# Three-product stick-breaking scores, with small moves around two square sums, eight decays and three normalizations

## The chip, the cores and the metric

One core of one Trainium2 chip runs the whole program. The metric is the device time of one execution in microseconds (us), lower is better. The core has TensorE (PE in the rows; its weight loads are PEld), VectorE (DVE), ScalarE (ACT), GpSimd (POOL) and SyncE (SP, which here only issues transfers). Each engine runs its own instructions in the order in which they were written; semaphores carry the dependences between engines.

## What is computed

Two blocks on 512 tokens of width 1024, batch 1, float32. The first has two sequence mixers and an MLP, the second is sparse attention (NSA). The parts near the change, cut from the reference:

```
# first block
h = rms_norm(x, norm_mix_g)
p = h @ w_in                      # q_a k_a v_a o_a i_a f_a q_b k_b v_b g_a g_b
...
qn, kn = head_rms_norm(q_b), head_rms_norm(k_b)        # 8 heads of 128
y = gates[:D] * y_a + gates[D:] * stick_breaking(qn, kn, v_b)
x = x + y @ w_out
x = x + square(relu(rms_norm(x) @ w_up)) @ w_down

def stick_breaking(q, k, v):      # per head
    z = q @ k.T / sqrt(128)       # the scores; only s < t counts
    log_keep = where(s < t, log_sigmoid(-z), 0)
    suffix   = reverse_cumsum(log_keep) - log_keep
    A = where(s < t, exp(log_sigmoid(z) + suffix), 0)
    return A @ v

# the other mixer, 8 heads of 64, has a decay per pair of positions:
#   P = exp(b_t - b_s + i_s - m_t) * (q . k)
```

The second block starts with a norm (the second of three that the change touches) and ends with an output projection whose input is turned in the same way (the third).

## The kernel before

Weights come in slabs of 1 MB (`w_raw`, two buffers) by SP. ACT writes a rounded copy of each slab (`split_hi`, L688, into `w_hi`) and DVE the remainder (`split_lo`, L696, into `w_lo`); both are in the type fp32r, which TensorE takes in one pass. Every large product is then three fp32r products: high by high, high by low, low by high. Activations are split in the same way (`act_hi`, `act_lo`). A product tile has 128 rows and 512 columns, and its two banks `ps_g` are used in turn; other work has `ps_z` and `ps_t`.

There is no scheduler. The order on each engine is the order in which the program writes it, so a wait at the head of an engine's queue holds all that stands behind it. Four places matter.

**First slabs (L1273 to L1324).** PE sums the first value slabs over eight steps (`first_step`) and then starts the next ones (`mm_half` on `N_VA + 2`), whose first tile goes to `ps_z` and needs the `act_evacuate` of the tile before (ACT, L883, `v_a<-ps_z`). ACT also makes the sums of squares of the four token blocks of x (`square_sum`, L1725), which wait for the transfers `x_sb<-in_x`. They lead over `sq_done` and DVE to `rstd`, `diag_ready` and the scaling of x.

**Decay heads (L1350 to L1391, loop over 8 heads).** Per head ACT writes `decay` (`decays`, L1780, four exponentials), POOL masks it (L2532), DVE multiplies it with the scores (L2195), and PE multiplies the result with the values (L1374). A head's slab for the next head is split in the same loop.

**Stick-breaking heads (L1418 to L1458, loop over 8 heads, `h`).** PE: the scores of head h into `ps_z` (L1428, four causal column blocks of 512, 384, 128 and 256, plain fp32), the values product of head h-1 (L1414), one gate tile of 24 products, half of the second one, the suffix sums (L1441 to L1454, from `sp_hi` and `sp_lo`), the rest of the second tile. ACT: Abs, Exp and Ln of the scores (L1860 to L1862, with a table load ahead of Ln), the rounded copy `sp_hi` (L1869), the gate's tanh (L891, table load ahead), the exponential `attn_b` (L1876), the second tanh. DVE: L2235, `sp_lo` (L2239), the gate product (L968), a minimum on `ps_z` in four parts (L2247), the gate product, and `normalize(h + 2)` (L2207), which gives the normalized q_b and k_b. Head 0 differs: PE computes its scores after three of the four tiles of the last value slab (`N_VB + 3`), and ACT has just evacuated the third of these (`v_b<-ps_g`, L883) and loaded the table of Exp (L1843).

**Three turned activations (`feature_tiles`, L782).** PE transposes four normalized token blocks (`xn` or `o_a`) into eight feature tiles of 512 columns, 128 columns per block (L789). Tiles 0 and 1 lie in `ps_g`, 2 to 7 in `ps_z` and `ps_t`. The last block is late. ACT then writes `act_hi` (`act_feature_tile`, L849) and DVE `act_lo` (`dve_feature_tile`, L862 or L860), tile by tile, and the next slab's first product needs both of tile 0.

Of the kernel before, what the change touches and what calls it, by code (L numbers as in the profile page):

```python
# [23 lines left out]
ALU = mybir.AluOpType  # L24
ACT = mybir.ActivationFunctionType
AX_X = mybir.AxisListType.X
F32 = mybir.dt.float32
F32R = mybir.dt.float32r

P = 128  # L30
# [143 lines left out]
def program(nc, a, out):  # L174

    with ExitStack() as ctx:
# [40 lines left out]
        y_lo = sb("y_lo", [P, KT, S], F32R, at=arena + 4 * K16)  # L217
        yb_f = sb("yb_f", [P, HB, S], at=arena + 3 * K16)
# [82 lines left out]
        m_bc = [sb("m_bc0", [P, S], at=tile_t_at + 2048), sb("m_bc1", [P, S], at=t1 + 7168 + 2048 * 3)]  # L301
        den_sum = sb("den_sum", [P, S - P], at=tile_t_at)
# [115 lines left out]
        b_sp = sem("b_sp")  # L418
        b_masked = sem("b_masked")
# [41 lines left out]
        gain_in = sem("gain_in")  # L461
        out_ready = sem("out_ready")
# [56 lines left out]
        BY_ACT = {"norm": 1, "conv": 1, "no": 1, "oa": 1, "ga": 1, "gb": 2, "up": 3, "nz": 1, "zw": 1}  # L519
# [23 lines left out]
        for n in range(N_ALL):  # L543
            taken_at[n] = tuple(taken)
            if n in norm_before:
                norm_tile_of[n] = len(kinds)
                take("norm")
                take("norm")
# [233 lines left out]
        def feature_tiles(pe, n, src, block_ready, between=None, before=None, late=None, halves=False):  # L782
# [4 lines left out]
            def turn(b, ks):  # L787
                for k in ks:
                    mm = nc.tensor.transpose(feature_bank(n, k)[:, b * P:(b + 1) * P],  # L789
                                             src(b)[:, k * P:(k + 1) * P], ident)  # L790
                    if b == TB - 1:
                        mm.then_inc(tile_ready if k < 2 else norm_done, 1)

            for j in range(TB - 1):
                block_ready(j)
                if j == 0 and before is not None:

                    wait_tile_free(pe, tile_of[before])
                    wait_tile_free(pe, tile_of[before] + 1)
                if late is None:  # L800
# [11 lines left out]
            for k in (0, 1):  # L812
                wait_bank(pe, t0 + k)
                for j in range(TB - 1):
                    turn(j, (k,))
            block_ready(TB - 1)
            turn(TB - 1, range(HALF_K))
# [24 lines left out]
        def act_feature_tile(act, n, k, which, gain):  # L842

            if k < 2:
# [3 lines left out]
            scale = 1.0 if gain is None else col(gain, k)  # L848
# [3 lines left out]
        def dve_feature_tile(dve, n, k, which, gain):  # L852
            t = norm_tile_of[n] + k
            if k < 2:
                after_act(dve, t, 1)
# [396 lines left out]
        def _(pe):  # L1252
# [165 lines left out]
            for h in range(HB):  # L1418
# [6 lines left out]
                pe.wait_ge(b_normed, 2 * h + 2)  # L1425
                for b in (0, 1, 3, 2):
                    at, w = CAUSAL_AT[b], CAUSAL_W[b]
                    mm = nc.tensor.matmul(ps_z[:, at:at + w], k_b[:, h, b * P:(b + 1) * P],  # L1428
                                          q_b[:, h, b * P:S], start=(b != 3), stop=True,
                                          skip_group_check=True)  # L1430
# [277 lines left out]
        def _(act):  # L1708
# [28 lines left out]
            for b in range(2):  # L1737
                square_sum(b)
            act_evacuate(act, N_VA + 1, 0)
            act_evacuate(act, N_VA + 1, 1)  # L1740
            square_sum(2)
            act_evacuate(act, N_VA + 1, 2)
            act_evacuate(act, N_VA + 1, 3)
# [990 lines left out]
```

## Time and profile before

| | |
|---|---|
| median of 3 runs | 1310.84 us (1310.53 to 1311.0) |
| the profiled execution | 1312.24 us |
| its span, first to last instruction | 1310.5 us |
| PE busy | 1297.0 us, 99% |
| DVE busy | 766.7 us, 59% |
| ACT busy | 690.2 us, 53% |
| POOL busy | 194.7 us, 15% |
| DMA | 130.72 MB, mean 100 GB/s |

An engine's busy share tells how much of the span it had an instruction in work. Matmuls are pipelined, so a product's duration is longer than the step to the next product's start; how long PE works is read from starts. The profiled execution took 1.4 us more than the median, and 1.7 us of it lie outside the span.

### The profile page before, as it was taken

To read this page: it belongs to the slowest core of one execution; us is meant where nothing else is said; L and a number is where in the kernel's file an instruction comes from. 1 tells how busy PE (TensorE), PEld (TensorE's weight loads), DVE (VectorE), ACT (ScalarE), POOL (GpSimd) and SP (SyncE) were. 2 spreads that over 40 slices of the span, in tenths; PEclk is the share of its full clock that TensorE was granted. 3 is DMA by queue.
4 is the path that set the end of the run, shared out by engine and by line. 5 is a ranking of instruction groups with operands and counts; after the bars stand their busy time and mean duration, and the time that the engine had idled before them with its cause. 6 is when DMAs were issued, how large, how long until landed. Compare 5 with 4: busy or idle time off the path is not lost.

```text
span 1310.5 us, 16447 instructions
## 1 busy us (share of the span) xinstructions
PE 1297.0 (99%) x6464; PEld 1055.5 (81%) x6464; DVE 766.7 (59%) x1184; ACT 690.2 (53%) x1070; POOL 194.7 (15%) x260
## 2 busy tenths in 40 slices
PE   8999999999999999999999999999999999999998
PEld 7787777787778887888888888788888888888886
DVE  4696443435544545595775958822157778786553
ACT  5547555357676334554635546544335667675332
POOL 0002332151000000000000000003712333431000
PEclk9999999999999999999999999999999999999999
DMA  8333221464111234143070430372612122231311
GB/s 311 90 107 119 81 81 65 111 189 120 65 41 56 97 97 165 60 142 115 1 250 8 150 107 1 97 229 81 142 35 79 60 96 73 67 104 52 118 65 65
DMA packets 64444, 130.72 MB, mean 100 GB/s; under 512 B 3999, under 2 KB 33695, under 8 KB 60272
## 3 DMA queue, kind: packets, MB, share of 16 engines
q1 hardware_dynamic: 58320, 110.81, 25.1%
q0 software_dynamic: 5904, 18.81, 5.9%
q8 instruction: 52, 0.85, 0.3%
q14 instruction: 24, 0.20, 0.1%
q10 hardware_dynamic: 144, 0.06, 0.0%
HBM read 126.77 MB, written 2.88 MB: 99 GB/s over the span
## 4 chain that ended last, share of the span: by engine, by line
PE 94%; DMA 2%; DVE 1%; issue 1%; ACT 0%; POOL 0%; SPq 0%; DVEq 0%; POOLq 0%
PE ps_g L728 39%; PE ps_g L751 16%; PE ps_z L751 7%; PE ps_t L1500 7%; PE ps_z L1500 5%; PE ps_z L1611 3%; PE ps_z L1649 3%; PE ps_t L1683 3%; PE ps_z L1428 1%; PE ps_t L1414 1%; PE ps_t L1374 1%; PE ps_t L1533 1%; DMA x_sb<-in_x 1%; PE ps_z L1454 1%; DMA w_raw<-in_w_in_t 1%
## 5 line engine op out<-in xcount | busy, mean ns | idle before, releaser
L728 PE MATMUL ps_g<-act_hi,w_hi 128*128 128x512 f32 x760 | 299.1, 394 | 1.3 <-DVE act_lo L862 0.9
L728 PE MATMUL ps_g<-act_hi,w_lo 128*128 128x512 f32 x760 | 296.0, 390 | 0.0
L728 PE MATMUL ps_g<-act_lo,w_hi 128*128 128x512 f32 x760 | 295.8, 389 | 0.0
L696 DVE TENSOR_TENSOR w_lo<-w_raw,w_hi 128x2048 fp32r<-128x2048 f32 x80 | 182.6, 2283 | 192.9 <-ACT w_hi L688 192.5
L688 ACT ACTIVATE w_hi<-w_raw 128x2048 fp32r<-128x2048 f32 x80 | 152.3, 1904 | 88.1 <-PE ps_g L751 47.9
L728 PEld LDWEIGHTS ps_g<-act_hi,w_hi 128*128 128x128 f32 x760 | 142.7, 188 | 32.6 <-issue 4.1
L728 PEld LDWEIGHTS ps_g<-act_hi,w_lo 128*128 128x128 f32 x760 | 142.7, 188 | 30.1
L728 PEld LDWEIGHTS ps_g<-act_lo,w_hi 128*128 128x128 f32 x760 | 142.8, 188 | 28.5
L751 PE MATMUL ps_g<-w_hi,act_hi 128*128 128x512 f32 x264 | 107.0, 405 | 0.7 <-DVE act_lo L860 0.7
L751 PE MATMUL ps_g<-w_hi,act_lo 128*128 128x512 f32 x264 | 103.2, 391 | 0.0
L751 PE MATMUL ps_g<-w_lo,act_hi 128*128 128x512 f32 x264 | 102.7, 389 | 0.0
L2625 POOL TENSOR_SCALAR cmp_in_k<-pairk,vec 128x124 f32<-128x124 f32 x16 | 13.5, 864 | 491.2 <-ACT pairk L917 491.2
L2007 ACT ACTIVATE probs<-probs,rneg 128x128 f32<-128x128 f32 (+3 forms) x128 | 70.4, 552 | 7.7 <-DVE rneg L2446 7.5
L688 ACT ACTIVATE w_hi<-down_raw 128x2048 fp32r<-128x2048 f32 x24 | 46.1, 1919 | 50.9 <-PE ps_t L1500 29.2
L696 DVE TENSOR_TENSOR w_lo<-down_raw,w_hi 128x2048 fp32r<-128x2048 f32 x24 | 55.0, 2290 | 8.0 <-ACT w_hi L688 8.0
L2645 POOL TENSOR_TENSOR q_parts<-qn,q_parts 64x512 fp32r<-64x512 f32 x32 | 41.3, 1289 | 117.6 <-ACT q_parts L1987 117.1
L899 ACT ACTIVATE ev_t<-ps_g 128x512 f32<-128x512 f32 x32 | 19.1, 597 | 74.9 <-PE ps_g L728 74.9
L751 PEld LDWEIGHTS ps_g<-w_hi,act_lo 128*128 128x128 f32 x264 | 49.5, 188 | 10.9
L751 PEld LDWEIGHTS ps_g<-w_hi,act_hi 128*128 128x128 f32 x264 | 49.7, 188 | 9.9 <-issue 1.1
L751 PEld LDWEIGHTS ps_g<-w_lo,act_hi 128*128 128x128 f32 x264 | 49.8, 188 | 9.1
L2442 DVE CUSTOM_DVE_ANT_0 probs<-ps_z,tile_t 128x128 f32<-128x128 f32 (+3 forms) x128 | 55.0, 485 | 3.1 <-PE ps_z L1611 3.1
L981 DVE TENSOR_TENSOR up_lo<-up_raw,up_hi 128x256 fp32r<-128x256 f32 (+1 forms) x32 | 17.8, 557 | 54.9 <-ACT up_hi L904 54.9
(389 smaller groups left out, 2486.9 us busy)
## 6 DMA issues: line engine op xcount, KB each, us to landing
w_raw<-in_w_in_t SPq DMA_DIRECT2D x30, 1024.0 KB, 4.9
w_raw<-in_nsa_w_in SPq DMA_DIRECT2D x20, 1024.0 KB, 5.1
w_raw<-in_w_up SPq DMA_DIRECT2D x16, 1024.0 KB, 5.5
down_raw<-in_w_down SPq DMA_DIRECT2D x16, 1024.0 KB, 5.3
tile_t<-bias_rev_dram POOLq DMA_DIRECT2D x32, 256.0 KB, 3.1
bc<-stat_rows_dram POOLq DMA_DIRECT2D x24, 256.0 KB, 6.3
w_raw<-in_w_out SPq DMA_DIRECT2D x4, 1024.0 KB, 5.1
w_raw<-in_nsa_w_out SPq DMA_DIRECT2D x4, 1024.0 KB, 5.0
```

The costliest lines, as they stand in the source:

```text
L688: nc.scalar.activation(slab_view(parts(n)[0], n), slab_view(raw(n), n), ACT.Copy).then_inc(hi_done, 1)
L696: nc.vector.tensor_tensor(slab_view(lo, n), slab_view(raw(n), n), slab_view(hi, n).bitcast(F32), ALU.subtract).then_inc(lo_done, 1)
L728: mm = nc.tensor.matmul(o, stationary, moving, start=(k == 0 and j == 0), stop=(k == KT - 1 and j == 2))
L751: mm = nc.tensor.matmul(bank(t), act[:, k, m], w[:, k - k0, :], start=(k == 0 and j == 0), stop=(k == KT - 1 and j == 2))
L899: nc.scalar.activation(ev_t[:, g, :], ps_g[:, g, :], ACT.Relu).then_inc(ev_act, 1)
L1500: mm = nc.tensor.matmul(down_bank(p, i), act[:, k, m], w[:, k, :], start=(first and k == 0 and j == 0), stop=(k == HALF_K - 1 and j == 2), ...
L1611: mm = nc.tensor.matmul(ps_z[:, at:at + w], q_parts[u % 2][:, b * P:(b + 1) * P], keys[u // 4 % 2][:, 0:w], start=(j == 0), stop=(j == 1))
L1649: mm = nc.tensor.matmul(ps_z[64 * e:64 * e + 64, CAUSAL + at * P:CAUSAL + 2 * P], values[:, s, g * DH:(g + 1) * DH], blocks[:, first:last: ...
L1683: mm = nc.tensor.transpose(ps_t[:, at:at + P], probs[u % 2][:, ROWS_AT[b] + s * P:ROWS_AT[b] + (s + 1) * P], ident)
L2007: ins = nc.scalar.activation(p, p, ACT.Exp, bias=rneg[:, u % 2, b:b + 1], accum_out=rsum[:, u % 2, b:b + 1])
L2442: ins = nc.vector.tensor_tensor_reduce(probs[u % 2][:, at:at + w], ps_z[:, at:at + w], tile_t[u % 2][:, S - w:S], 1.0, -3.0e38, ALU.add, A ...
L2645: nc.gpsimd.tensor_tensor(q_parts[u % 2][64 - half:128 - half, :], qn[half:half + 64, 4 * (h // 8) + h % 4, :], q_parts[u % 2][half:half + ...
```

## The change

It has four parts.

1. **Scores.** The normalized q_b and k_b of a head are split into fp32r parts (`qk_hi` on ACT into two new tiles `q_b_hi` and `k_b_hi`; `qk_lo` on DVE, in place of q_b and k_b), and the scores become three fp32r products per column block in place of one fp32 product. PE waits for `b_qk_lo` where it waited for `b_normed`. In the same loop the weight splits move: ACT's from the start of a head to behind `sp_hi`, DVE's to behind the minimum.
2. **First values.** ACT's four evacuations of the first value tiles stand between the square sums, the first of them ahead of all.
3. **Decays ahead of splits.** In decay heads 1 to 7 ACT writes the decays before it splits the next slab, and DVE multiplies them before its part of the split.
4. **Norm tiles in two pieces.** Feature tile 0's first three blocks are turned earlier; ACT copies these 384 columns while the last block is still missing, and the last 128 afterwards. PE waits for the first copy before it writes the last block.

```diff
@@ tiles and tables @@
+        q_b_lo = sb("q_b_lo", [P, HB, S], F32R, at=arena + 3 * K16)
+        k_b_lo = sb("k_b_lo", [P, HB, S], F32R, at=arena + 4 * K16)
+        q_b_hi = sb("q_b_hi", [P, S], F32R, at=tile_t_at)
+        k_b_hi = sb("k_b_hi", [P, S], F32R, at=tile_t_at + 2048)
-        BY_ACT = {"norm": 1, "conv": 1, "no": 1, "oa": 1, "ga": 1, "gb": 2, "up": 3, "nz": 1, "zw": 1}
+        BY_ACT = {"norm0": 2, "norm": 1, "conv": 1, "no": 1, "oa": 1, "ga": 1, "gb": 2, "up": 3, "nz": 1, "zw": 1}
...
@@ feature_tiles (PE) @@
+                if j == TB - 2:
+
+                    wait_bank(pe, t0)
+                    for i in range(TB - 1):
+                        mm = turn(i, (0,))
+                    mm.then_inc(norm_early, 1)
...
-            for k in (0, 1):
-                wait_bank(pe, t0 + k)
-                for j in range(TB - 1):
-                    turn(j, (k,))
+            wait_bank(pe, t0 + 1)
+            for j in range(TB - 1):
+                turn(j, (1,))
             block_ready(TB - 1)
+            after_act(pe, t0, 1)
             turn(TB - 1, range(HALF_K))
...
@@ act_feature_tile (ACT) @@
+            if k == 0:
+
+                act.wait_ge(norm_early, which)
+                nc.scalar.activation(act_hi[:, k, 0:S - P], feature_bank(n, k)[:, 0:S - P], ACT.Copy,
+                                     scale=scale).then_inc(ev_act, 1)
+                tile_done(act, norm_tile_of[n])
+                nc.scalar.activation(act_hi[:, k, S - P:S], feature_bank(n, k)[:, S - P:S], ACT.Copy,
+                                     scale=scale).then_inc(ev_act, 1)
+                return
...
@@ stick-breaking heads (PE) @@
-                pe.wait_ge(b_normed, 2 * h + 2)
+                pe.wait_ge(b_qk_lo, 2 * h + 2)
                 for b in (0, 1, 3, 2):
                     at, w = CAUSAL_AT[b], CAUSAL_W[b]
-                    mm = nc.tensor.matmul(ps_z[:, at:at + w], k_b[:, h, b * P:(b + 1) * P],
-                                          q_b[:, h, b * P:S], start=(b != 3), stop=True,
-                                          skip_group_check=True)
+                    keys, queries = slice(b * P, (b + 1) * P), slice(b * P, S)
+                    for j, (k, q) in enumerate(((k_b_hi[:, keys], q_b_hi[:, queries]),
+                                                (k_b_hi[:, keys], q_b_lo[:, h, queries]),
+                                                (k_b_lo[:, h, keys], q_b_hi[:, queries]))):
+                        mm = nc.tensor.matmul(ps_z[:, at:at + w], k, q, start=(b != 3 and j == 0), stop=(j == 2),
+                                              skip_group_check=True)
...
@@ first values (ACT) @@
-            for b in range(2):
-                square_sum(b)
             act_evacuate(act, N_VA + 1, 0)
+            square_sum(0)
             act_evacuate(act, N_VA + 1, 1)
+            square_sum(1)
             square_sum(2)
             act_evacuate(act, N_VA + 1, 2)
+            square_sum(3).then_inc(sq_done, 1)
             act_evacuate(act, N_VA + 1, 3)
-            square_sum(3).then_inc(sq_done, 1)
...
@@ decay heads (ACT; DVE's split_lo moves in the same way) @@
-                split_hi(act, n + 1)
                 if h:
                     act.wait_ge(a_ssq, h)
                     decays(h)
+                split_hi(act, n + 1)
...
@@ stick-breaking heads (ACT) @@
+            def qk_hi(h):
+
+                act.wait_ge(b_normed, 2 * h + 2)
+                if h:
+                    act.wait_ge(b_z, h)
+                for src, dst in ((q_b, q_b_hi), (k_b, k_b_hi)):
+                    nc.scalar.copy(dst[:], src[:, h, :]).then_inc(b_hi, 1)
+
+            qk_hi(0)
             for h in range(HB):
                 n = N_OA + h
-                if h:
-                    split_hi(act, n + 1)
...
-                if h == 0:
-                    split_hi(act, n + 1)
+                split_hi(act, n + 1)
                 act_evacuate(act, n, 0)
+                if h + 1 < HB:
+                    qk_hi(h + 1)
                 act.wait_ge(b_min, h + 1)
...
@@ stick-breaking heads (DVE) @@
+            def qk_lo(h):
+                for e, (src, dst, hi) in enumerate(((q_b, q_b_lo, q_b_hi), (k_b, k_b_lo, k_b_hi))):
+                    dve.wait_ge(b_hi, 4 * h + e + 1)
+                    nc.vector.tensor_tensor(dst[:, h, :], src[:, h, :], hi[:].bitcast(F32), ALU.subtract)\
+                        .then_inc(b_qk_lo, 1)
+
+            qk_lo(0)
```

On ACT, at the entry to the stick-breaking heads, this stands before (`v_b` is a value tile's evacuation, `rstd<-cst` a one-element Exp that loads the table, `sp_t<-ps_z` the Abs of head 0):

```order
L883 ACTIVATE v_b<-ps_z 128x512 [waits tile_ready] x2
L883 ACTIVATE v_b<-ps_g 128x512 [waits tile_ready]
L1843 ACT_TABLE_LOAD
L1843 ACTIVATE rstd<-cst 1x1
L1860 ACTIVATE sp_t<-ps_z 128x1280 [waits stats_out,b_z,act_order]
```

and this now:

```order
L905 ACTIVATE v_b<-ps_z 128x512 [waits tile_ready] x2
L905 ACTIVATE v_b<-ps_g 128x512 [waits tile_ready]
L1868 ACT_TABLE_LOAD
L1868 ACTIVATE rstd<-cst 1x1
L1880 CAST q_b_hi<-q_b 128x512 [waits b_normed,act_order]
L1880 CAST k_b_hi<-k_b 128x512
L1892 ACTIVATE sp_t<-ps_z 128x1280 [waits stats_out,b_z]
```

The two copies of head 0 stand behind the evacuation of the third value tile and the table load, ahead of the Abs.

On DVE, from head 0's gate product to head 1's `L2235` (`ps_z<-ps_z,cst` is the minimum, `w_lo` the split of a slab), this stands before:

```order
L968 SCALAR_TENSOR_TENSOR y_f<-ev_t,y_f 128x512 [waits a_y,ev_act]
L2247 TENSOR_TENSOR ps_z<-ps_z,cst 128x128 [waits b_sfx]
L2247 TENSOR_TENSOR ps_z<-ps_z,cst 128x128 x3
L968 SCALAR_TENSOR_TENSOR y_f<-ev_t,y_f 128x512 [waits a_y,ev_act]
L2207 SCALAR_TENSOR_TENSOR q_b<-q_b,gq_s,bc_89 128x512 [waits bc_in4]
L2207 SCALAR_TENSOR_TENSOR k_b<-k_b,vec,bc_90 128x512 [waits bc_in5]
L696 TENSOR_TENSOR w_lo_56<-w_raw_52,w_hi_54 128x2048 [waits hi_done]
```

and this now:

```order
L990 SCALAR_TENSOR_TENSOR y_f<-ev_t,y_f 128x512 [waits a_y,ev_act]
L2281 TENSOR_TENSOR ps_z<-ps_z,cst 128x128 [waits b_sfx]
L2281 TENSOR_TENSOR ps_z<-ps_z,cst 128x128 x3
L2261 TENSOR_TENSOR q_b_lo<-q_b,q_b_hi 128x512 [waits b_hi]
L2261 TENSOR_TENSOR k_b_lo<-k_b,k_b_hi 128x512 [waits b_hi]
L702 TENSOR_TENSOR w_lo_57<-w_raw_53,w_hi_55 128x2048 [waits hi_done]
L990 SCALAR_TENSOR_TENSOR y_f<-ev_t,y_f 128x512 [waits a_y,ev_act]
```

Between the minimum and the second gate product there are now the two remainders for the next head's scores and the slab's split.

## Rows read from the trace of the kernel before

**Rows 1.** The page: busy time of each engine, and the chain's shares.

```profile
PE 1297.0 (99%) x6464; PEld 1055.5 (81%) x6464; DVE 766.7 (59%) x1184; ACT 690.2 (53%) x1070; POOL 194.7 (15%) x260
...
PE 94%; DMA 2%; DVE 1%; issue 1%; ACT 0%; POOL 0%; SPq 0%; DVEq 0%; POOLq 0%
```

**Rows 2.** Waits of PE: total us, times, longest us.

```profile
PE ps_g L728 <- DVE act_lo L862: 1.8, 2, 0.9
PE ps_g L751 <- DVE act_lo L860: 0.7, 1, 0.7
```

**Rows 3.** Timeline, first values: start us, us, engine, line, operation, [idle before].

```profile
29.29 1.07 ACT L883 ACTIVATE v_a<-ps_z 128x512 f32<-128x512 f32 x2
...
28.26 0.39 PE L1273 MATMUL ps_g<-w_lo,act_hi 128*128 128x512 f32 x1
30.02 0.47 PE L751 MATMUL ps_z<-w_hi,act_hi 128*128 128x512 f32 x1 [1.36 <-ACT v_a L883]
```

**Rows 4.** Timeline, decay head 1: ACT, DVE, PE.

```profile
121.28 1.92 ACT L688 ACTIVATE w_hi<-w_raw 128x2048 fp32r<-128x2048 f32 x1
...
127.64 1.49 DVE L2195 SCALAR_TENSOR_TENSOR decay<-ps_z,decay 128x1280 f32<-128x1280 f32 x1 [2.12 <-POOL decay L2532]
...
128.30 0.39 PE L728 MATMUL ps_g<-act_hi,w_lo 128*128 128x512 f32 x1
129.19 0.70 PE L1374 MATMUL ps_t<-decay,v_a 128*128 128x512 f32 x1 [0.51 <-DVE decay L2195]
```

**Rows 5.** Timeline of PE, head 1: the scores and the values behind them.

```profile
295.62 2.32 PE L1428 MATMUL ps_z<-q_b,k_b 128*128 128x512 f32 x8
297.78 2.32 PE L1414 MATMUL ps_t<-attn_b,v_b 128*128 128x512 f32 x8
```

**Rows 6.** Timeline of PE: suffix sums of head 1, fp32r pieces.

```profile
308.15 0.39 PE L1441 MATMUL ps_z<-sp_hi,tri_r 128*128 128x512 f32 x1
...
308.60 0.51 PE L1447 MATMUL ps_z<-sp_hi,tri_r 128*128 128x384 f32 x3
...
309.70 0.57 PE L1447 MATMUL ps_z<-sp_lo,tri_r 128*128 128x384 f32 x3
```

**Rows 7.** Timeline at the entry to head 0: PE, then ACT.

```profile
277.04 2.32 PE L1428 MATMUL ps_z<-q_b,k_b 128*128 128x512 f32 x8
...
277.24 0.60 ACT L883 ACTIVATE v_b<-ps_g 128x512 f32<-128x512 f32 x1 [2.12 <-PE ps_g L751]
277.86 1.28 ACT L1843 ACT_TABLE_LOAD   x1
...
279.45 1.24 ACT L1860 ACTIVATE sp_t<-ps_z 128x1280 f32<-128x1280 f32 x1
```

**Rows 8.** Two lines' instructions: ns min/median/max, first and last start.

```profile
L1731 ACT CAST act_hi<-x_t x8: 609/618/621, 45.6 to 61.4; 128x512 fp32r<-128x512 f32 x8
...
L2109 DVE TENSOR_TENSOR act_lo<-x_t,act_hi x8: 678/682/692, 46.8 to 62.1; 128x512 fp32r<-128x512 f32 x8
```

**Rows 9.** Timeline, second part of head 1: ACT, DVE, PE.

```profile
308.31 0.60 ACT L891 ACTIVATE ev_t<-ps_g 128x512 f32<-128x512 f32 x1
311.99 1.24 ACT L1876 ACTIVATE attn_b<-ps_z 128x1280 f32<-128x1280 f32 x1 [3.08 <-DVE ps_z L2247]
...
311.06 0.89 DVE L2247 TENSOR_TENSOR ps_z<-ps_z,cst 128x128 f32<-128x128 f32 x4 [1.42 <-PE ps_z L1454]
...
313.64 2.32 PE L1428 MATMUL ps_z<-q_b,k_b 128*128 128x512 f32 x8
```

**Rows 10.** Timeline of ACT, first norm: tiles 0 and 1.

```profile
514.55 1.27 ACT L849 ACTIVATE act_hi<-ps_g,vec 128x512 fp32r<-128x512 f32 x2 [1.41 <-PE ps_g L789]
```

**Rows 11.** Timeline of PE at both ends; windows with granted clock (PEclk), DMA, GB/s.

```profile
1.75 4.27 PE L1299 MATMUL ps_t<-k_diag 128*128 128x128 f32 x20 [1.75 <-DVE k_diag L2082]
...
1304.70 0.39 PE L751 MATMUL ps_z<-w_hi,act_lo 128*128 128x512 f32 x1
...
1309.40:1310.50 1.10, 0.00 (x0) 0.00 (x0) 0.00 (x0) 0.00 (x0) 0.00 (x0) 0.50 0.22 82
```

More of the change, by code:

```diff
@@ L418, in program @@
         b_sp = sem("b_sp")
+        b_qk_lo = sem("b_qk_lo")
         b_masked = sem("b_masked")
@@ L461, in program @@
         gain_in = sem("gain_in")
+        norm_early = sem("norm_early")
         out_ready = sem("out_ready")
@@ L546, in program @@
                 norm_tile_of[n] = len(kinds)
-                take("norm")
+                take("norm0")
                 take("norm")
@@ L792, in turn @@
                         mm.then_inc(tile_ready if k < 2 else norm_done, 1)
+                return mm
             for j in range(TB - 1):
@@ L842, in act_feature_tile @@
         def act_feature_tile(act, n, k, which, gain):
+            scale = 1.0 if gain is None else col(gain, k)
+            if k == 0:
[6 more added lines that the diff above has]
+                return
             if k < 2:
@@ L847, in act_feature_tile @@
                 act.wait_ge(norm_done, 6 * (which - 1) + k - 1)
-            scale = 1.0 if gain is None else col(gain, k)
             nc.scalar.activation(act_hi[:, k, :], feature_bank(n, k), ACT.Copy,
@@ L854, in dve_feature_tile @@
             if k < 2:
-                after_act(dve, t, 1)
+                after_act(dve, t, 2 - k)
             else:
@@ L2190, in _ @@
             for h in range(HA):
-                if h:
-                    split_lo(dve, N_QB + h + 1)
                 dve.wait_ge(a_scores, h + 1)
@@ L2196, in _ @@
                                                ALU.mult).then_inc(a_probs, 1)
-                if h == 0:
-                    split_lo(dve, N_QB + h + 1)
+                split_lo(dve, N_QB + h + 1)
                 if h < HA - 1:
@@ L2226, in _ @@
             split_lo(dve, N_OA)
+            def qk_lo(h):
[4 more added lines that the diff above has]
+            qk_lo(0)
             for h in range(HB):
                 n = N_OA + h
-                if h:
-                    split_lo(dve, n + 1)
                 dve.wait_ge(b_ln, h + 1)
@@ L2237, in _ @@
                 for p, part in enumerate(SP_PARTS):
-                    dve.wait_ge(b_hi, 2 * h + p + 1)
+                    dve.wait_ge(b_hi, 4 * h + 2 + p + 1)
                     nc.vector.tensor_tensor(sp_lo[:, part], sp_t[:, part], sp_hi[:, part].bitcast(F32),
                                             ALU.subtract).then_inc(b_lo, 1)
-                if h == 0:
-                    split_lo(dve, n + 1)
                 dve_evacuate(dve, order, n, 0)
@@ L2248, in _ @@
                 ins.then_inc(b_min, 1)
+                if h + 1 < HB:
+                    qk_lo(h + 1)
+                split_lo(dve, n + 1)
                 dve_evacuate(dve, order, n, 1)
```

## The prediction, written before the change was run

> **What bounds the kernel now.** I read the page first: PE is busy in 99% of the span, and the chain that ended last runs through PE for 94% of it [rows 1]. So only two things count: what PE's own instructions take, and the few places where PE stands still. The view of PE's waits names these places. Two kinds concern the change: the wait for `act_lo` behind the turned activations, 1.8 us in two places and 0.7 us in one [rows 2], and two single waits that the timeline shows better, since a product's duration covers some 0.16 us of a gap. One product of 512 columns follows the next by 0.225 us (308.15 to 308.60 is two of them [rows 6]). In the first values the last product of one group starts at 28.26 and the next at 30.02 [rows 3], so PE stood still for 1.76 - 0.23 = 1.53 us. In decay head 1 the step is 128.30 to 129.19 [rows 4], a stall of 0.66 us. DVE and ACT are loaded by half. They matter where PE waits for them, or where the change makes PE wait.
>
> **First values.** PE waits there for ACT's first evacuation, which starts at 29.29 [rows 3], behind two square sums. Its tile was ready long before: PE ends the four tiles three products at a time, so the first tile's last product began nine products before 28.26, at 26.2. With the evacuation ahead of the square sums it is done by about 27.3, before PE wants the bank. The second evacuation now waits for one square sum, but PE needs that bank only one tile and one small group later. The stall goes whole: **-1.5 us**. What is next late there? The diagonal of rstd, which hangs on the last square sum; that sum comes no later than now, since an evacuation moves from ahead of it to behind it. If the DMA or a later wait took the gain back it would be 0; it cannot be more than 1.53.
>
> **Decays.** In decay head 1 ACT splits a slab from 121.28 for 1.92 us [rows 4] and only then comes to the decays. POOL's mask and DVE's product follow, and DVE ends at 127.64 + 1.49 = 129.13, where PE waits. With the split behind, that chain is 1.9 us earlier and the 0.66 us are covered. Heads 2 to 7 have no gap there, since head 1 alone carries a table load in this chain, so nothing more is won. The split moves back by about 3 us, but its slab is wanted a whole head later, which hides it. **-0.65 us**, between 0 and -0.66.
>
> **Norm tiles.** The first product behind the turned blocks waits for ACT and DVE of tile 0. ACT's two copies of 512 columns take 1.27 together, the first from 514.55 [rows 10]. With 384 columns copied ahead, ACT has 128 left. ACT takes 0.618 us for 512 columns [rows 8] and 1.24 for 1280 [rows 9], 0.0008 us a column, so 384 fewer save 0.31 us. DVE's part stays whole. Three places: **-0.95 us**. PE's new wait, ahead of the last block's transposes, holds nine of its instructions; the first three blocks' copy (about 0.6 us) starts when three early transposes are done and runs beside nine others of 0.11 us each, so it ends about where PE asks. Bounds: 0 if that wait costs 0.3 each time, -1.0 if nothing.
>
> **Scores.** Now 295.62 to 297.78, 2.16 us a head [rows 5]. In future: three products of 512 columns, 0.675 us, and nine of 384, 128 and 256, 2304 columns. The nearest row is the suffix sums' nine pieces of fp32r, 2048 columns from 308.60 to 309.70, 1.10 us [rows 6]; with 256 columns more at 0.225/512 each it is 1.21. Together 1.89 us, 0.27 less a head, for eight heads **-2.2 us**. By columns alone it would be 3840 x 0.00044 = 1.69 us (-3.8 us in all); if the short pieces cost so much that nothing is won, 0. I take the middle, since the row is of the same shape and type.
>
> **The price of the parts, head 0.** This is the step that decides. PE now starts head 0's scores at 277.04 and waits for nothing [rows 7]. In the change they need `b_qk_lo`: two copies on ACT and two subtractions on DVE. The order shows the copies behind ACT's evacuation of the third value tile. That tile is PE's very last work ahead of the scores, so the evacuation starts only at 277.24, and the table load stands behind it from 277.86 for 1.28 us [rows 7]. ACT is free at about 279.4 (it starts the Abs at 279.45). Then: two copies of 512 columns at 0.618 [rows 8], overlapping by 0.1, to 280.55; the second subtraction at 0.68 [rows 8] starts behind the first and ends at 281.35; PE starts at about 281.45. Behind the waiting instruction on PE stands everything, the fourth value tile and the first gate tile among it, though neither needs the scores. A stall of 281.45 - 277.04 = **+4.4 us**, between 4.1 and 4.7. Nothing later in head 0 gives it back, since all its waits hang on the scores.
>
> The Trainium skill (ScalarE: Activation LUTs, "What ACT_TABLE_LOAD costs") gives a table switch 1283 ns for the load and some 1380 ns more for a drain. The trace shows the load alone at this place, since the next evacuation ends just ahead of it and the Abs starts 0.31 us behind it [rows 7]; by the page's sum the stall would be 5.8 us and the time 1311.4.
>
> **The price of the parts, heads 1 to 7.** Two copies (1.14 us) and two subtractions (1.3 us) a head lie on ACT and DVE beside PE. In head 1 ACT's tanh starts at 308.31; the slab's split of 1.92 us [rows 4] now comes ahead of it, less 0.4 because the Abs no longer waits behind a split, so it starts at about 309.8 and ends at 310.4. The copies follow to 311.6, in time for the exponential, which starts at 311.99 [rows 9]. DVE's gate product (0.7 us) behind the tanh ends at 311.1, where the minimum starts at 311.06 [rows 9]. All of PE's work comes 0.27 us earlier, so the minimum is late by 0.1 to 0.3. It takes 0.89, then the exponential 1.24 and, on DVE, the subtractions 1.3: both end about 313.2 to 313.4 in this head's time, and PE wants them at 313.64 - 0.27 = 313.37 [rows 9]. It is a tie. I take **+0.1 us** for the seven heads, between 0 and 0.3 each.
>
> **Sum.** -1.5 - 0.65 - 0.95 - 2.2 + 4.4 + 0.1 = -0.8 us. The profiled execution of before took 1312.24 with a span of 1310.5, 1.4 above the median of its three runs; the sum is made in its span, so I expect a span of 1309.7, and on the median 1310.84 - 0.8 = **1310.0 us**.
>
> **Rivals.**
>
> *Faster: no stall at head 0.* The scores' parts would have to be ready by 277.04, and the rest of the sum gives 1310.84 - 5.2 = 1305.6. Against it stands the order on ACT, which no dependence can change. Chance 6%.
>
> *Clock.* In this trace PE's granted clock is 1.00 until just before 1309.40, where it is 0.50; PE's last product began at 1304.70, so it fell some 4.3 us after PE had ended [rows 11]. The stall at head 0 is about as long. At the kernel's start the twenty warm-up pieces took 4.27 us [rows 11], most of it at the lower level; if the clock falls in the stall, a similar stretch of products runs at half speed and loses up to 1.9 us: 1311.9. The Trainium skill (TensorE: Matmul & The Clock Gate, Part 1) has idleness as what throttles the engine and activity as what releases it; by that rule this rival is real. Chance 18%, and within 0.2% of before.
>
> *Slower: the tie is lost in heads 1 to 7.* One mechanism: ACT's split ahead of the tanh ends late, DVE's gate product then holds the minimum, and both the exponential and the remainders come behind PE's demand. It speaks for it that four estimates meet within 0.2 us; against it, that the Abs starts earlier. Beyond 0.5 us a head it adds 3.5 us and the kernel is slower by over 0.2%; at 0.6 us a head the time is 1310.0 + 4.1 = 1314.1. Chance 8%.
>
> *First values give nothing back.* The 1.5 us stall reappears at the scaling of x or at a slab's transfer, and the time is 1311.5. Against it: everything between 30 and 60 us waits for PE. Chance 6%.
>
> **How the numbers follow.** Forecast 60%, clock 18%, slower tie 8%, first values 6%, faster 6%, something else 2%. A difference of 0.2%, 2.6 us, is about what a measurement of this kernel can tell from no change. Forecast, clock and first values lie within it: same 0.84. Faster 0.07: the first rival and a tail of the scores' lower bound. Slower 0.09: the tie, and the clock with part of it. Range 1308.2 to 1312.1: below, the scores by columns alone (-1.6 more); above, the clock's 1311.9 and the ties of 0.3 us a head (1310.0 + 2.0).
>
> **What would show it.** In the profile after: PE's wait for `v_a` at 30 us and for `decay` in head 1 are gone. The first product of each norm waits about 0.6 and 0.4 us, not 0.9 and 0.7. The scores start to values start is 1.9 us. PE has a wait of some 4.4 us for `k_b_lo` near 275 us, which would be its longest, and none above 0.3 us in heads 1 to 7. The clock is below 1.00 behind that wait in the second rival. The prediction is wrong if that wait is under 3 us, or if a second wait of over 1 us appears anywhere.

## The result, and the profile after

The changed kernel takes **1312.95 us** (median of 20 runs, 1312.61 to 1314.2); the kernel before, on the same chip, 1310.92 (20 runs, 1310.12 to 1312.37). The ratio is 1.0015 (95% interval 1.0009 to 1.0021): about 2.0 us slower. Forecast were 1310.0 us and a range of 1308.2 to 1312.1, so the time lies outside the range, and it moved the other way: +2.0 where -0.8 was forecast. It is still within the 0.2% that the prediction called no change.

The profiled execution took 1314.2 us with a span of 1312.5, the longest of the 20; the half-clock stretch below accounts for that (experiment 8 has a second look). First the page of the changed kernel (busy times and shares, then the chain that ended last), which answers to [rows 1]:

```profile
span 1312.5 us, 16560 instructions
PE 1297.3 (99%) x6496; PEld 1061.0 (81%) x6496; DVE 775.4 (59%) x1200; ACT 700.4 (53%) x1089; POOL 202.9 (15%) x260
PE 97%; DVE 1%; ACT 1%; issue 0%; DMA 0%; DVEq 0%; SPq 0%; ACTq 0%
```

PE is still busy for 99% of the span, and the page alone would say that nothing happened. The view of PE's waits says more (us in total, times, longest); it answers to [rows 2]:

```profile
PE ps_z L1454 <- DVE k_b_lo L2261: 4.3, 1, 4.3
PE ps_t L1321 <- DVE k_diag L2115: 1.8, 1, 1.8
PE ps_g L734 <- DVE act_lo L884: 1.1, 2, 0.6
PE ps_g L795 <- DVE xn L1099: 1.0, 2, 0.6
PE ps_z L1295 <- ACT act_hi L1742: 0.5, 1, 0.5
PE ps_g L757 <- DVE act_lo L882: 0.4, 1, 0.4
```

The waits for `act_lo` fell from 1.8 and 0.7 us to 1.1 and 0.4, as forecast. Those for `v_a` and for the decay are gone. On top stands the new one, 4.3 us for `k_b_lo`. The timeline of PE, ACT and DVE at that place (start, duration, instruction, and in brackets the idle time before it) answers to [rows 7]:

```profile
274.32 0.39 PE L757 MATMUL ps_g<-w_hi,act_lo 128*128 128x512 f32 x1
274.75 0.60 ACT L905 ACTIVATE v_b<-ps_g 128x512 f32<-128x512 f32 x1 [2.12 <-PE ps_g L757]
275.36 1.28 ACT L1868 ACT_TABLE_LOAD   x1
276.66 0.20 ACT L1868 ACTIVATE rstd<-cst 1x1 f32<-1x1 f32 x1
276.89 0.62 ACT L1880 CAST q_b_hi<-q_b 128x512 fp32r<-128x512 f32 x1
277.42 0.61 ACT L1880 CAST k_b_hi<-k_b 128x512 fp32r<-128x512 f32 x1
277.54 0.69 DVE L2261 TENSOR_TENSOR q_b_lo<-q_b,q_b_hi 128x512 fp32r<-128x512 f32 x1 [6.65 <-ACT q_b_hi L1880]
278.15 0.69 DVE L2261 TENSOR_TENSOR k_b_lo<-k_b,k_b_hi 128x512 fp32r<-128x512 f32 x1
278.98 0.76 PE L1454 MATMUL ps_z<-q_b_hi,k_b_hi 128*128 128x512 f32 x1 [4.27 <-DVE k_b_lo L2261]
279.55 0.63 PE L1454 MATMUL ps_z<-q_b_lo,k_b_hi 128*128 128x512 f32 x1
279.97 0.63 PE L1454 MATMUL ps_z<-q_b_hi,k_b_lo 128*128 128x512 f32 x1
```

The chain is the one the prediction wrote down, link by link: evacuation, table load, two copies, two subtractions. PE's last product is at 274.32 instead of 276.82, since this execution is 2.5 us ahead by then; the next could have followed 0.23 later and comes at 278.98, a stall of 4.43. DVE had waited 6.65 us for ACT. Note the last three rows: scores of 512 columns follow each other by 0.57 and 0.42 us and last 0.76, 0.63 and 0.63. In head 1 the first two of them start at 300.28 and 300.51 and last 0.39 and 0.40. The windows view tells why (PE busy, PEld, DVE, ACT, POOL with instruction counts, then the granted clock, the DMA share and GB/s):

```profile
275.00:278.00 3.00, 0.00 (x0) 0.00 (x0) 0.46 (x1) 2.94 (x5) 3.00 (x5) 1.00 0.97 220
278.00:279.00 1.00, 0.02 (x1) 0.05 (x1) 0.84 (x2) 0.03 (x1) 0.05 (x1) 0.73 0.97 397
279.00:280.00 1.00, 1.00 (x3) 0.81 (x4) 0.00 (x0) 0.00 (x0) 0.00 (x0) 0.50 0.98 406
...
284.00:285.00 1.00, 1.00 (x4) 0.81 (x3) 0.00 (x0) 0.97 (x2) 0.00 (x0) 0.50 0.03 12
285.00:286.00 1.00, 1.00 (x5) 0.78 (x5) 0.00 (x0) 0.98 (x2) 0.00 (x0) 0.85 0.00 0
```

The granted clock is 0.50 (1.2 GHz) from 278.5 (0.73 is the mean of a microsecond in which it falls at 0.46) to 285.3, 6.8 us. It fell while PE had been idle for some 3.9 us. Of that stretch 6.3 us hold products, each at half speed: about 3.1 us lost. This is the rival "Clock", in this execution at more than its price of 1.9.

### The profile page after: what moved, and what is told of

It is laid out like the page before. It is cut to its first block, busy times and chain, and to the rows that moved or that the text cites. A ratio compares the mean times of both kernels' runs of the same rounds, so it can differ in the third digit from the quotient of the medians.

```text
span 1312.5 us, 16560 instructions
## 1 busy us (share of the span) xinstructions
PE 1297.3 (99%) x6496; PEld 1061.0 (81%) x6496; DVE 775.4 (59%) x1200; ACT 700.4 (53%) x1089; POOL 202.9 (15%) x260
## 4 chain that ended last, share of the span: by engine, by line
PE 97%; DVE 1%; ACT 1%; issue 0%; DMA 0%; DVEq 0%; SPq 0%; ACTq 0%
PE ps_g L734 40%; PE ps_g L757 16%; PE ps_z L757 7%; PE ps_t L1525 7%; PE ps_z L1525 5%; PE ps_z L1636 3%; PE ps_z L1674 3%; PE ps_t L1708 3%; PE ps_z L1454 1%; PE ps_t L1436 1%; PE ps_t L1396 1%; PE ps_t L1558 1%; PE ps_z L1479 1%; PE ps_z L1384 1%; PE ps_z L1295 1%; PE ps_g L1295 1%
```

## The experiments

Two questions were open. Is the low clock the stall's doing, or that of the new products? And the profiled executions, one against the other, show every part's gain; do the medians show it too?

**1. Remove the stall, keep the rest.** On ACT and on DVE, head 0's copies and remainders go ahead of the slab's split; their inputs are ready long before, for DVE ends the second head's normalization at 262.8 us.

```diff
+            qk_hi(0)
             split_hi(act, N_OA)
             for i in (0, 1, 2):
                 act_evacuate(act, N_VB + 3, i)
...
-            qk_hi(0)
...
+            qk_lo(0)
             split_lo(dve, N_OA)
-            qk_lo(0)
```

> The changed kernel with head 0's two copies on ACT moved ahead of the split of the slab N_OA, and its two subtractions on DVE moved ahead of the same slab's remainder; nothing else differs. The stall theory: PE's 4.4 us wait ahead of head 0's scores is gone, and with it the 6.8 us at granted clock 0.5 that the changed kernel shows behind it. All parts keep what they gave (first values -1.6, decay -0.66, norms -0.96, scores 8 x -0.27): 1310.9 - 5.4 = 1305.5 us, clock 1.00 throughout. Rival A (the low clock near 280 us comes from the new kind of products, not from the idle time): the stall goes, the slow stretch stays, 1305.5 + 2.8 = 1308.3. Rival B (the loss is spread over heads 1 to 7 or the norms): 1308.5 with no slow stretch.

Measured: **1306.73 us** (1306.47 to 1307.43), ratio 0.9965 (0.9951 to 0.9979) against 1310.98 for before on this chip. No wait for `k_b_lo`, and the granted clock is 1.00 behind the place:

```profile
276.00:278.00 2.00, 2.00 (x14) 1.88 (x13) 0.00 (x0) 1.94 (x4) 2.00 (x4) 1.00 0.91 170
278.00:280.00 2.00, 2.00 (x11) 1.65 (x10) 0.00 (x0) 1.97 (x2) 0.95 (x2) 1.00 0.99 379
```

The same scores now run at full clock, so rival A (the kind of product) falls. This kernel beats both others. In the early place the two remainders last 1.77 us each on DVE, not 0.69, and nothing waits for them. Yet the time is 1.2 us above the 1305.5 that the parts should give, and that was not expected.

**2. The scores alone.** The kernel before with the scores' part of the change: this core and all the splits, copies and subtractions that go with it.

```diff
-                pe.wait_ge(b_normed, 2 * h + 2)
+                pe.wait_ge(b_qk_lo, 2 * h + 2)
...
-                    mm = nc.tensor.matmul(ps_z[:, at:at + w], k_b[:, h, b * P:(b + 1) * P],
-                                          q_b[:, h, b * P:S], start=(b != 3), stop=True,
-                                          skip_group_check=True)
+                    for j, (k, q) in enumerate(((k_b_hi[:, keys], q_b_hi[:, queries]),
+                                                (k_b_hi[:, keys], q_b_lo[:, h, queries]),
+                                                (k_b_lo[:, h, keys], q_b_hi[:, queries]))):
```

> The kernel before with the scores' part of the change alone. Stall theory: scores 8 x -0.27 = -2.2, stall +4.4, lost clock behind it about +2.8: 1310.9 + 5.0 = 1315.9 us, with a clock of 0.5 for 6 to 7 us behind the wait for k_b_lo. Rival A (low clock from the kind of product) gives the same total; its low clock would also show behind the scores of other heads. Rival C (the clock fell only because PE came to that place 3 us earlier in the changed kernel): full clock, 1310.9 + 2.2 = 1313.1.

Measured: 1315.68 us (1315.23 to 1316.14), ratio 1.0033 (1.0020 to 1.0046), 4.7 above before. In its profiled execution the clock is at 0.50 again behind the stall:

```profile
280.00:282.00 2.00, 2.00 (x6) 1.71 (x7) 0.00 (x0) 0.00 (x0) 0.00 (x0) 0.50 0.99 395
```

So this part, alone, costs 4.7 us as the change has it. The clock falls though none of the other parts brings PE to the place early (its last product before is at 275.23, 0.9 us later than in the changed kernel), so rival C falls too.

**3. The three other parts alone.** The changed kernel with all of the above undone (the same diff the other way round).

> The changed kernel with the scores' part undone: first values, decays and norm tiles alone. By the sum of what the trace of the changed kernel shows: -1.6 - 0.66 - 0.96 = -3.2, so 1307.7 us, clock 1.00 throughout. If one of the three parts costs something elsewhere that the traces did not show (a later wait, the transfer of a slab), 1308.5 or more.

Measured: 1308.83 us (1308.34 to 1309.24), ratio 0.9982 (0.9973 to 0.9991): 2.15 us won, where 3.2 were expected. The missing 1.1 us are those missing in experiment 1 too. Against experiment 1, same chip, the scores give 1306.73 - 1308.83 = -2.10, as forecast (-2.2). So what falls short is among first values, decays and norms.

**4. Fill the stall.** In head 0 PE gets 18 products whose sums are overwritten.

```diff
+                if h == 0:
+                    for _ in range(18):
+                        nc.tensor.matmul(ps_z[:, 0:512], tri_r[:], act_hi[:, 0, :], start=True, stop=True,
+                                         skip_group_check=True)
                 pe.wait_ge(b_qk_lo, 2 * h + 2)
```

> The changed kernel with 18 extra products of 512 columns on PE ahead of its wait for head 0's parts; their sums are overwritten by the scores, which start their banks anew. 18 x 0.227 = 4.1 us of the 4.4 us stall are filled, and nothing else moves: the scores start at the same time. Stall theory with the clock as its second price: the clock stays at 1.00, the time is 1305.5 + 4.4 = 1309.9 us, 3.0 below the changed kernel. Rival A (low clock from the kind of product): the slow stretch stays and the time is that of the changed kernel, 1312.9. Rival D (ACT and DVE hold the scores back for another reason than their queues, and the extra products push them further): above 1313.

Measured: 1311.36 us (11 runs, 1310.65 to 1311.69), ratio 1.0000 (0.9992 to 1.0009). The scores start as late as in the changed kernel (278.8 against 278.98), and the clock stays up:

```profile
278.00:279.00 1.00, 0.89 (x4) 0.43 (x4) 0.73 (x2) 0.00 (x0) 0.00 (x0) 1.00 1.01 422
279.00:280.00 1.00, 1.00 (x6) 0.87 (x6) 0.00 (x0) 0.00 (x0) 0.00 (x0) 1.00 0.97 401
```

This takes the two prices apart. The stall itself is 1311.36 - 1306.73 = 4.6 us (4.4 to 4.5 in the traces); the clock is 1312.95 - 1311.36 = **1.6 us** on the median, or 2.0 if one goes by the two ratios, since the chips differed. All 20 runs of the changed kernel are above 1312.6, and all 11 of this one below 1311.7, so by the times the clock falls in every execution; both profiled executions of the changed kernel show it (experiment 8 is the second). But 1.6 is half of what the profiled execution had lost.

**5. The first values alone.**

```diff
-            for b in range(2):
-                square_sum(b)
             act_evacuate(act, N_VA + 1, 0)
+            square_sum(0)
             act_evacuate(act, N_VA + 1, 1)
+            square_sum(1)
             square_sum(2)
             act_evacuate(act, N_VA + 1, 2)
+            square_sum(3).then_inc(sq_done, 1)
             act_evacuate(act, N_VA + 1, 3)
-            square_sum(3).then_inc(sq_done, 1)
```

> The kernel before with the first values' part alone (each evacuation on ACT ahead of the square sums that stood in front of it). Theory P (what was predicted): the 1.53 us stall near 30 us is in every execution and the part gives 1.5: ratio 0.9988, 1309.4 us. Theory V (the stall depends on when x_sb arrives): the profiled execution of before had x_sb at 26.96 and a stall of 1.53, the scores' kernel, whose first values are those of before, had it at 25.61 and a gap of under 0.3. Then the part gives 1.5 in some executions and next to nothing in the others, on the median 0.3 to 0.8: 1310.2 to 1310.7, with a narrower spread of its times than before's 2.0 us, since the upper ones of them go. By the runs so far: the three other parts together gave 2.15, less 0.66 and 0.96 leaves 0.5.

Measured: 1310.78 us (11 runs, 1310.18 to 1311.18) against 1311.22 (21 runs, 1310.27 to 1314.93), ratio 0.9994 (0.9985 to 1.0003). It gives 0.4 on the median. The interval of the ratio, -2.0 to +0.4 us, excludes neither nothing nor 1.5; the single runs say more. Those with the part lie within 1.0 us, from 1310.18. Those of before spread over 2.1 from 1310.27 up to 1312.35, and one is at 1314.93. A part that won 1.5 in every execution would have moved the lowest time too, and it moved by 0.1; the part takes away the upper ones.

**6. Fill half of the stall.** As experiment 4 with 9 products, so that 2.3 us stay idle (`range(9)`).

> As the run with 18 extra products ahead of PE's wait, with 9: 2.04 us of the stall are filled and some 2.4 us stay idle. The scores start at the same time. If the clock falls with any idle stretch of this size, the time is that of the changed kernel, 1312.9. If a stretch of 2.4 us doesn't bring it down, it is that of the 18 products, 1311.4, with clock 1.00 behind it. Between the two (falls in some executions) 1312.

Measured: 1312.73 us (1311.17 to 1313.28), ratio 1.0009 (1.0000 to 1.0018). Three of the 11 runs are at 1311.2 to 1311.7, where those with 18 products are, and eight at 1312.4 to 1313.3, where those of the changed kernel are. The profiled execution (1311.17) is one of the three, and its clock is 1.00 from 276 to 282:

```profile
278.00:280.00 2.00, 1.09 (x5) 0.96 (x6) 0.85 (x2) 0.05 (x1) 0.00 (x0) 1.00 0.96 369
```

None of the eight was profiled, but the mean clock recorded with each is 0.997 to 0.999, and that of the three 0.999 or 1.0. So, by times and mean clocks, an idle stretch of 2.3 us brings the clock down in some executions and not in others; one of 4.4 us did in all.

**7. The kernel before, once more.** No edit.

> The kernel before, unchanged, for a second look at its first 35 us. Theory V: where x_sb arrives by 25.7, PE's step near 30 us is 0.3 or less and the span is 1308.7 to 1309.3; where it arrives near 26.9 the step is 1.76 and the span near 1310.5. Theory P: step 1.76 whatever the arrival.

Measured: 1311.18 us, span 1309.4. ACT's timeline in this execution, and behind it PE's step, answer to [rows 3]:

```profile
25.86 1.06 ACT L1725 ACTIVATE xn<-x_sb 128x1024 f32<-128x1024 f32 x1 [0.88 <-DMA x_sb<-in_x]
28.17 1.07 ACT L883 ACTIVATE v_a<-ps_z 128x512 f32<-128x512 f32 x2
28.25 0.39 PE L1273 MATMUL ps_g<-w_lo,act_hi 128*128 128x512 f32 x1
28.90 0.47 PE L751 MATMUL ps_z<-w_hi,act_hi 128*128 128x512 f32 x1 [0.26 <-ACT v_a L883]
```

In the execution that the prediction read, the same square sum starts later, and the evacuation with it, at 29.29 [rows 3]:

```profile
26.96 1.06 ACT L1725 ACTIVATE xn<-x_sb 128x1024 f32<-128x1024 f32 x1 [2.32 <-DMA x_sb<-in_x]
```

In experiment 2, whose first values are those of before, it starts earlier than in both:

```profile
25.61 1.06 ACT L1733 ACTIVATE xn<-x_sb 128x1024 f32<-128x1024 f32 x1 [2.47 <-DMA x_sb<-in_x]
28.24 0.39 PE L1278 MATMUL ps_g<-w_lo,act_hi 128*128 128x512 f32 x1
28.47 0.47 PE L756 MATMUL ps_z<-w_hi,act_hi 128*128 128x512 f32 x1
```

All three end PE's first group at 28.24 to 28.26. What differs is when the transfer of `x_sb` lets ACT begin: at 25.61, 25.86 and 26.96, and PE's step is 0.23 (no stall), 0.65 and 1.76 us. The stall is the transfer's arrival, passed on by the two square sums. What counts is when it arrives, not how long ACT has waited: the execution without a stall has the longest wait, 2.47 us. The second look at before ends 1.06 us earlier than the first, and at 28.90 it is 1.12 ahead.

**8. The changed kernel, once more.** No edit.

> The changed kernel, unchanged, for a second look at the clock behind the stall. Its profiled execution was the longest of 20 (1314.2 against a median of 1312.95) with 6.83 us at granted clock 0.5. If the low stretch has one length, it is 6.8 us again and the span is near 1312.5; if its length varies, a span near 1311.1 goes with 3 to 4 us of low clock, worth 1.5 to 1.9 us, and then the clock is worth about 1.6 on the median, as the difference to the run with 18 extra products says (1312.95 - 1311.36).

Measured: 1312.83 us, span 1311.1. The same windows as above:

```profile
278.00:279.00 1.00, 0.00 (x0) 0.00 (x0) 0.92 (x2) 0.11 (x1) 0.00 (x1) 1.00 1.01 389
279.00:280.00 1.00, 0.94 (x4) 0.79 (x5) 0.00 (x0) 0.00 (x0) 0.00 (x0) 0.81 1.01 397
280.00:281.00 1.00, 1.00 (x5) 1.00 (x4) 0.00 (x0) 0.00 (x0) 0.00 (x0) 0.50 1.03 361
...
283.00:284.00 1.00, 1.00 (x6) 0.76 (x5) 0.00 (x0) 0.97 (x2) 0.00 (x0) 0.98 0.26 94
```

The same stall, but the clock falls at 279.6, when PE is already at work again, and is back at 283.0: 3.4 us at half speed, 1.7 us lost, not 3.1. The spans differ by 1.4 us. From PE's last value product ahead of head 0's scores to head 1's first score it is 24.59 us here (274.41 to 299.00), 22.99 in experiment 4 (274.21 to 297.20) and 25.96 in the first look (274.32 to 300.28): 1.6 and 3.0 us for the clock. So the price of the clock has more than one size in the same kernel, and the smaller one fits the median.

**9. Work of its own in the stall.** The fourth value tile needs none of the parts and comes ahead of PE's wait.

```diff
+                if h == 0:
+                    mm_half(pe, N_VB + 3, 3)
                 pe.wait_ge(b_qk_lo, 2 * h + 2)
...
                 if h:
                     sb_values(h - 1)
-                else:
-                    mm_half(pe, N_VB + 3, 3)
```

> The changed kernel with the fourth value tile's 12 products (2.72 us), which needs none of the scores' parts, ahead of PE's wait in head 0 instead of behind the scores. The scores start at the same time, so the stall falls from 4.4 to 1.7 us and nothing else moves: -2.7. Clock theory: an idle stretch of 2.4 us let the clock fall in most executions but not in all (the run with 9 extra products), one of 0.3 us in none; with 1.7 it falls seldom, so another -1.6 on the median: 1312.95 - 2.7 - 1.6 = 1308.6 us. If it falls in every execution: 1310.2.

Measured: 1310.77 us (11 runs, 1310.15 to 1311.02), ratio 0.9994 (0.9985 to 1.0003): 2.2 us above what was expected. The clock is not it, 1.00 throughout in the profiled execution. PE's waits between 270 and 300 us tell:

```profile
PE ps_z L1456 <- DVE k_b_lo L2261: 1.5, 1, 1.5
PE ps_z L1472 <- DVE sp_lo L2275: 0.7, 1, 0.7
PE ps_g L734 <- ACT v_b L905: 0.4, 1, 0.4
PE ps_z L1456 <- ACT attn_b L1909: 0.2, 1, 0.2
```

The stall went to 1.6 (the 1.5 of this view and what a product's duration covers), nearly the 1.7 expected, and three waits came up behind it: two in the same head, and one ahead of head 1's scores. They show 1.3 us here and cost 2.1: from the third value tile's last product to head 1's scores it is 22.25 us (274.12 to 296.37) against 18.52 in experiment 1 (275.02 to 293.54), 3.7 more, of which 1.6 are the first stall. That is nearly the whole 2.2. The value tile had been the cover under which ACT and DVE turned head 0's scores into `sp`. Moved ahead of the scores it fills one hole and leaves another.

**10. The tie in heads 1 to 7.** Experiment 1's kernel with the next slab's split at the start of these heads again, as before has it, on ACT and DVE.

```diff
             for h in range(HB):
                 n = N_OA + h
+                if h:
+                    split_hi(act, n + 1)
                 act.wait_ge(b_z, h + 1)
...
-                split_hi(act, n + 1)
+                if h == 0:
+                    split_hi(act, n + 1)
                 act_evacuate(act, n, 0)
```

> The kernel without the stall (copies and remainders of head 0 early), with the split of the next slab on ACT and DVE put back to the start of heads 1 to 7, where the kernel before has it. It prices the tie that was forecast for these heads. In the trace of the kernel without the stall the last of head 1's exponential and remainders ends at 311.07 and PE asks near 311.3, so there is 0.2 to 0.3 us to spare. The split (1.92 us) ahead of the Abs delays ACT's chain by about 0.4 us and DVE's by about as much: PE then waits 0.1 to 0.3 us a head, +0.7 to +2 in all, 1307.4 to 1308.7. If the heads have more slack than that reading says: 1306.7, no wait for attn_b or k_b_lo.

Measured: 1306.9 us (1306.57 to 1307.14), ratio 0.9967 (0.9955 to 0.9979), the same as experiment 1. PE waits for nothing between 270 and 450 us. The heads have more slack than the forecast's four close estimates said, and in heads 1 to 7 moving the split was not needed.

**11. Decays and norms alone.** The kernel before with these two parts; for the decays:

```diff
             for h in range(HA):
                 n = N_QB + h
-                split_hi(act, n + 1)
                 if h:
                     act.wait_ge(a_ssq, h)
                     decays(h)
+                split_hi(act, n + 1)
```

> The kernel before with the decays' and the norms' parts alone. By the traces: -0.66 (decay head 1) and 3 x -0.32 (norms), -1.6 us, ratio 0.9988, in every execution, since neither hangs on a transfer: the spread of before, 2 us, stays. If the median gain of the first values is near 0.4, as their run alone showed, this and that run together give the 2.15 of all three.

Measured: 1309.37 us (11 runs, 1308.45 to 1310.16), ratio 0.9987 (0.9979 to 0.9996): -1.6 us as expected, and before's spread stays, 1.7 us. With the first values' 0.4 that makes 2.0 of the 2.15 of experiment 3. Its first values are again those of before, and `x_sb` comes early:

```profile
24.79 1.06 ACT L1742 ACTIVATE xn<-x_sb 128x1024 f32<-128x1024 f32 x1 [1.40 <-DMA x_sb<-in_x]
```

PE's step there is 0.23 us (28.17 to 28.40). So of four profiled executions with the old order two had no stall, one 0.4 us and one 1.5; in all nine with the new order the step is 0.22 or 0.23.

## Why the prediction was wrong, point by point

**Two steps failed.** The first values' term, -1.5, measured -0.4; and the sum has no term for the clock, which cost 1.6 to 2.0 us. The forecast is 2.95 us low by the two together. Either alone would have left the time inside the range: 1311.1 with the first, 1311.6 to 1312.0 with the second.

**Which engine and which places: right.** PE bounds both kernels, and the wait behind ACT's table load came where and as it was described.

**First values, -1.5: the term that was mis-sized.** Profile against profile it came out (-1.6 by 28.42, where the second group begins in the changed kernel, against 30.02 [rows 3]). On the median it is -0.4. The step that failed is the one that took a stall from one execution and put it, whole, against the median: "The stall goes whole". That execution took 1312.24, 1.4 above its median. The prediction named this difference and then subtracted on the median as if every execution had the same stall. The trace held the warning, a wait on a transfer at the root of the stall (the row of experiment 7 with 2.32 us for `x_sb`), but the prediction read only the evacuation's row and not what ACT had waited for. Error: 1.1 us. The intervals of the single experiments are about as wide as this error; what carries it is that experiments 1, 3, 5 and 11 agree on the medians, and the four traces with the old order.

**Decays -0.65 and norms -0.95: right.** In the traces -0.66 and three times -0.32; together -1.6 in experiment 11. In the changed kernel's decay head 1 the split (122.80) comes behind the decays and PE is not held (compare [rows 4]):

```profile
120.97 1.93 ACT L1805 ACTIVATE decay<-m_bc,u_col 128x512 f32<-128x512 f32 x4
122.80 1.90 ACT L694 ACTIVATE w_hi<-w_raw 128x2048 fp32r<-128x2048 f32 x1
124.11 1.49 DVE L2226 SCALAR_TENSOR_TENSOR decay<-ps_z,decay 128x1280 f32<-128x1280 f32 x1 [9.30 <-POOL decay L2569]
126.80 2.32 PE L1396 MATMUL ps_t<-decay,v_a 128*128 128x512 f32 x8
```

**Scores, -0.27 a head: right.** In the changed kernel's next head they start at 300.28 and the values at 302.20, 1.92 us where [rows 5] had 2.16. Head 1's period is 17.77 us (300.28 to 318.05) where it was 18.02, 0.25 shorter; experiments 1 and 3 give -2.1 for the eight. The suffix sums' short pieces were the right row to cost short products by; by columns alone it would have been 1.69.

```profile
300.28 0.39 PE L1454 MATMUL ps_z<-q_b_hi,k_b_hi 128*128 128x512 f32 x1
300.51 0.40 PE L1454 MATMUL ps_z<-q_b_lo,k_b_hi 128*128 128x512 f32 x1
...
302.20 1.34 PE L1436 MATMUL ps_t<-attn_b,v_b 128*128 128x512 f32 x3
```

**Stall at head 0, +4.4: right**, 4.43. The Trainium skill (ScalarE: Activation LUTs, "What ACT_TABLE_LOAD costs") adds a drain of some 1380 ns to the load; here the load starts 0.01 us behind the evacuation's end (274.75 + 0.60) and the next instruction 0.02 us behind the load's (275.36 + 1.28, then 276.66), so the trace doesn't agree. The stall that the prediction worked out from the page, 5.8 us, was not seen.

**Tie in heads 1 to 7, +0.1: 0.** In head 1 of the changed kernel the exponential ends at 317.81 and `k_b_lo` at 317.73, and PE asks at 318.05, with 0.24 us to spare (compare [rows 9]). Experiment 10 shows that even with the split back in its place nothing waits.

```profile
316.57 1.24 ACT L1909 ACTIVATE attn_b<-ps_z 128x1280 f32<-128x1280 f32 x1 [0.53 <-DVE ps_z L2281]
317.04 0.69 DVE L2261 TENSOR_TENSOR k_b_lo<-k_b,k_b_hi 128x512 fp32r<-128x512 f32 x1
318.05 0.39 PE L1454 MATMUL ps_z<-q_b_hi,k_b_hi 128*128 128x512 f32 x1
```

**The clock, a rival at 18% and nothing in the sum: it happened in every run.** This is the larger of the two errors. The mechanism was right, and the price (up to 1.9; measured 1.6 to 2.0 on the median) in part by luck. It was taken from the twenty pieces at the kernel's start, of which [rows 11] has only the 4.27 us together; the windows view gives 1.00 as the granted clock there, and the lower level can be read only from the pieces' starts, 0.21 us apart until 5.33 and 0.11 after. Behind the stall the low stretch was 6.8 us in one trace and 3.4 in the other, and 1.9 lies between what they lost. Its chance was too low. The only row on it had the clock falling some 4.3 us after PE's last product [rows 11], and a stall of 4.4 was forecast beside it. Two nearly equal numbers should have given a chance near a half. There is no one point either: the runs show it falling after 3.9 us idle (278.5) in one execution and at 279.6, with PE at work again, in another, and in most but not all with 2.3 us of idleness. The Trainium skill (TensorE: Matmul & The Clock Gate, Part 1) has idleness throttle the engine and activity release it; the runs agree: an idle PE lost the clock, a PE kept busy with sums that nobody read did not.

**The sum with these terms.** -0.4 - 1.6 - 2.1 + 4.6 + 1.6 to 2.0 = +2.1 to +2.5, against 2.0 measured. In the prediction's own terms: 1310.0 + 1.1 (first values) + 1.6 to 2.0 (clock) = 1312.7 to 1313.1. Experiment 2 has the scores' terms without the others: 4.7 + 2.1 - 4.6 leaves 2.2 us for the clock. The range missed because it let these two happen one at a time. (Its lower end is 0.2 off its own sum: 1310.0 - 1.6 is 1308.4, not 1308.2.)

## What to carry to other kernels

Trace a stall back to its root before it is subtracted: if the root is a transfer, its length can differ from one execution to the next (here 0 to 1.5 us), and one profile doesn't give its median; a few more show the spread. A stall of some us on TensorE can have two prices, its own length (here 4.4 us) and a stretch of products at half clock behind it (here another 1.6 us); dummy products in the stall took the second one off and so measured it. When new preparatory work hangs on an engine's queue, look where its inputs are ready: here the copies could go ahead of the table load (experiment 1, 0.9965), and filling the hole with later work moved most of the hole (experiment 9: 2.7 us filled, 2.1 us opened behind).

## What was not expected of the hardware

The same stall in the same kernel brought 6.8 us of half clock in one execution (278.5 to 285.3) and 3.4 us in another (279.6 to 283.0), and 2.3 us of idleness brought it in 8 of 11 runs by their times. What sets the moment of the fall is open; no run separated it from the start of the program. The transfer of `x_sb` let ACT begin at 24.79, 25.61, 25.86 or 26.96 us with the same work ahead of it, and this alone moved PE's next group by up to 1.5 us.
